# One head's squares, root and scaling placed earlier on ScalarE in the tail of an mLSTM stage

## What is computed

```python
h = mlstm_scan(q, k, vh, i_f, f_f) + flip(mlstm_scan(flip(q), flip(k), flip(vh), flip(i_b), flip(f_b)))
mu = h.mean(-1, keepdims=True)
var = jnp.square(h - mu).mean(-1, keepdims=True)
hn = ((h - mu) * lax.rsqrt(var + LN_EPS)).transpose(0, 2, 1, 3).reshape(B, S, M_WIDTH)
return jax.nn.sigmoid(o_pre) * hn * gn_w
...
y_a = mlstm_branch(...) @ w_a
y_b = dilated_attention(qkv_a, slopes) @ w_b
return (jax.nn.sigmoid(g_a) * y_a + jax.nn.sigmoid(g_b) * y_b) @ w_out
```

## Time and profile before

| | us |
|---|---|
| median of 3 runs | 3447.99 (3446.64 to 3450.39) |
| the profiled execution | 3447.72 |
| its span in the trace | 3446.0 |
| PE busy | 3372.9 (98%) |
| DVE, ACT, POOL busy | 1505.9, 1362.1, 1394.3 (44%, 40%, 40%) |
| mean busy share of the DMA engines | 37.4% (the main queue) |

### The profile page before, as it was taken

The page is one execution under the profiler, slowest core; times in us unless marked ns, Lnnn a source line. Parts: engine busy times, 40 slices in busy tenths (PEclk is TensorE's granted clock), DMA queues, the critical chain, the costliest instruction groups (busy, mean ns, idle before and its releaser), DMA issues.

```text
span 3446.0 us, 39148 instructions
## 1 busy us (share of the span) xinstructions
PE 3372.9 (98%) x15938; PEld 2715.8 (79%) x15938; DVE 1505.9 (44%) x2280; ACT 1362.1 (40%) x2322; POOL 1394.3 (40%) x749
## 2 busy tenths in 40 slices
PE   7999999999999999999999999999999999999999
PEld 5887777887888788777787888876678887778887
DVE  3436663344332343666326433556555402543320
ACT  3545454234232444446323422254632324642321
POOL 2333434444444433344344444442344444134443
PEclk9999999999999999999999999999999999999999
DMA  6334212544554333421244465432135433123332
GB/s 225 104 113 133 62 55 58 153 137 141 177 169 114 109 104 111 135 62 49 84 142 135 147 183 152 111 95 61 49 116 177 139 95 106 37 62 104 98 92 74
DMA packets 566994, 385.31 MB, mean 112 GB/s; under 512 B 13607, under 2 KB 504311, under 8 KB 566815
## 3 DMA queue, kind: packets, MB, share of 16 engines
q1 hardware_dynamic: 564574, 379.58, 37.4%
q10 hardware_dynamic: 2240, 3.25, 0.3%
HBM read 379.27 MB, written 2.10 MB: 111 GB/s over the span
## 4 chain that ended last, share of the span: by engine, by line
PE 92%; DVE 3%; ACT 2%; POOL 1%; DMA 0%; issue 0%; SPq 0%; DVEq 0%; ACTq 0%; POOLq 0%
PE ps L179 91%; PE ps L183 2%; DVE H L154 0%; DVE NUM L146 0%; ACT UF L138 0%; ACT whi L142 0%; DMA W<-in_w_ada 0%; POOL wlo L146 0%; SPq L176 0%; DVE G L163 0%; ACT ox L138 0%; POOL UL L146 0%; ACT L138 0%; DVE HV L150 0%; ACT UH L142 0%
## 5 line engine op out<-in xcount | busy, mean ns | idle before, releaser
L146 POOL TENSOR_TENSOR wlo<-raw,whi 128x1024 fp32r<-128x1024 f32 (+1 forms) x540 | 1256.8, 2336 | 1822.5 <-ACT whi L142 1747.1
L179 PE MATMUL ps<-UH,whi 128*128 128x512 f32 x2656 | 1054.5, 397 | 11.4 <-ACT UH L138 5.6
L179 PE MATMUL ps<-UL,whi 128*128 128x512 f32 x2656 | 1036.1, 391 | 4.0 <-POOL UL L146 3.2
L179 PE MATMUL ps<-UH,wlo 128*128 128x512 f32 x2656 | 1037.6, 391 | 0.5 <-POOL wlo L146 0.5
L142 ACT ACTIVATE whi<-raw 128x1024 fp32r<-128x1024 f32 (+1 forms) x540 | 548.6, 1026 | 744.9 <-PE ps L179 354.4
L179 PEld LDWEIGHTS ps<-UH,whi 128*128 128x128 f32 x2656 | 500.4, 188 | 134.3 <-ACT UH L138 11.4
L179 PEld LDWEIGHTS ps<-UL,whi 128*128 128x128 f32 x2656 | 499.8, 188 | 114.9 <-POOL UL L146 6.6
L179 PEld LDWEIGHTS ps<-UH,wlo 128*128 128x128 f32 x2656 | 500.7, 189 | 107.9 <-issue 3.8
L179 PE MATMUL ps<-GH,whi 128*128 128x512 f32 x704 | 275.3, 391 | 0.0
L179 PE MATMUL ps<-GH,wlo 128*128 128x512 f32 x704 | 274.2, 389 | 0.0
L179 PE MATMUL ps<-GL,whi 128*128 128x512 f32 x704 | 274.0, 389 | 0.0
(11 more groups left out here) (366 smaller groups left out, 4133.2 us busy)
## 6 DMA issues: line engine op xcount, KB each, us to landing
raw<-in_w_in SPq DMA_DIRECT2D x168, 512.0 KB, 3.9
raw<-in_w SPq DMA_DIRECT2D x120, 512.0 KB, 5.3
raw<-in_ada_w SPq DMA_DIRECT2D x96, 512.0 KB, 4.9
raw<-in_w_ada SPq DMA_DIRECT2D x80, 512.0 KB, 4.8
raw<-in_ffn_w_gate SPq DMA_DIRECT2D x44, 512.0 KB, 3.9
raw<-in_ffn_w_up SPq DMA_DIRECT2D x44, 512.0 KB, 3.9
raw<-in_ffn_w_down SPq DMA_DIRECT2D x32, 512.0 KB, 3.9
raw<-in_ev_w_in SPq DMA_DIRECT2D x20, 512.0 KB, 3.8
```

Of the source, the lines that this page charges most:

```text
L146: return self.e.tensor_tensor(o, a, b, op).then_inc(*self.done(*keys))
L179: m = self.e.matmul(o, l, r, start=start, stop=stop)
```

## The change

On ACT, the squares and the root of head 3 are issued right behind that head's `hf`, in sub-step 0 of `it == 4`, ahead of the sigmoids of `og` 5, `ga` 0 and `gb` 0. Heads 0 to 2 keep their place. On DVE the wait for the root, the reciprocal and the scaling of head 3 are written in sub-step 0 instead of 2.

```diff
+        def spread(h):
+            if h:
+                a.wait_ge(*on("dve", "hn", lay, h - 1))
+            for tb in range(4):
+                a.wait_ge(*on("dve", "hv", lay, h, tb))
+                a.af(T["SQ"][:, tb, :], T["HV"][:, tb, :], ACT.Square, ("hq", lay, h), accum_out=T["RS"][:, tb:tb + 1])
+            a.wait_ge(*on("act", "hq", lay, h))
+            a.af(T["RS"], T["RS"], ACT.Sqrt, ("hd", lay, h), scale=1.0 / 256, bias=EPS_LN)
...
                         a.af(T["HV"][:, tb, :], ps(("n", lay, h, tb))[:, 0:256], ACT.Identity, ("hf", lay, h, tb),
                              scale=DN[:, tb:tb + 1])
+                    if h == 3:
+                        spread(h)
...
-                if sub == 1 and h >= 0:
-                    if h:
-                        a.wait_ge(*on("dve", "hn", lay, h - 1))
-                    for tb in range(4):
-                        a.wait_ge(*on("dve", "hv", lay, h, tb))
-                        a.af(T["SQ"][:, tb, :], T["HV"][:, tb, :], ACT.Square, ("hq", lay, h),
-                             accum_out=T["RS"][:, tb:tb + 1])
-                    a.wait_ge(*on("act", "hq", lay, h))
-                    a.af(T["RS"], T["RS"], ACT.Sqrt, ("hd", lay, h), scale=1.0 / 256, bias=EPS_LN)
+                if sub == 1 and 0 <= h < 3:
+                    spread(h)
...
-                if sub == 2 and h >= 0:
+                if sub == (2 if it < 4 else 0) and h >= 0:
                     v.wait_ge(*on("act", "hd", lay, h))
```

## The result

| | before | changed |
|---|---|---|
| median of the runs, us | 3447.97 (3444.92 to 3451.29, 6 runs) | 3427.5 (3425.13 to 3429.23, 6 runs) |
| profiled execution, us | 3447.72 | 3429.23 |
| its span, us | 3446.0 | 3427.5 |

The ratio is 0.994, with a 95% interval of 0.9927 to 0.9952: clearly faster, by 20.5 us between the medians. The forecast was 3427.9, with 20.07 us as the sum of the terms. That the median comes within 0.4 us of it is luck: the interval leaves 16.6 to 25.2 us for the gain.

The account below looks back on a forecast made before the run. The prediction took PE, busy for 98% of the span, to bound the kernel. Savings of 15.12 + 1.58 + 3.37 = 20.07 us off 3447.72 gave 3427.65, stated as 3427.9 for the median, with a range of 3424.5 to 3434.

Parts of the forecast that it names:

- Step 1: From gb 0's last matmul to the first transpose, 7.79 us becomes 0.23 per layer: 15.12 us saved.
- Step 2: From the first transpose to og 6's first matmul, 1.62 us becomes 0.83 per layer: 1.58 us saved.
- Step 3: Block og 6's 24 matmuls fall from 7.01 and 7.42 us to 5.53: 3.37 us saved.
- Step 4: Early squares on ACT make og 5's sigmoid 1.2 us late; gb 0 needs its bank with 3.4 us slack: cost 0.
- Step 5: Roundings queued behind on ACT and POOL: POOL's two parts end near 561.1, PE reaches og 6 at 565.0: cost 0.
- Step 6: DVE's four scalings end at 554.8, PE asks at 564.2: slack 9.4 us, no delay from POOL counted.
- Step 7: DVE's YA and first gate products could each be held by one POOL part, at most 2.34 us: cost 0.
- a loss at the first block with w_a: Gain partly given back where PE reads YAL: 1.8 us wait, twice, giving 3431.5; chance 0.06.
- a clock that does not return: PE's clock does not return or falls elsewhere: 15.1 us saved, 3432.9; chance 0.04.
- another wait in the old one's place: Another PE wait, on a bank or DVE's queue, ends just as late: no change, 3448; chance 0.03.
- The slower one: Squares waiting for DVE's joining block ACT's queue, PE waits at gb 0; loses past 13.4 us of block: 3455; chance 0.02.

Follow-up runs that it names:

- the blocked run: The changed kernel with ACT waiting, ahead of head 3's squares, until PE has made block ga 0: 3442.38 us, ratio to before 0.9986.
- the squares between the sigmoids: The changed kernel with head 3's squares and root moved between the sigmoids of ga 0 and gb 0: 3428.84 us, ratio 0.9942.
- both edits together: The kernel before with PE's transposes behind og 6 and ACT's rounding for ga 1 behind og 6's sigmoid: 3428.99 us, ratio 0.9947.
- the one-layer run: The changed kernel with head 3's squares and root early in layer 0 alone: 3436.98 us, ratio 0.996.

## Why the prediction was right

The forecast, that the stall ends in both layers and everything behind moves up, held, and each term of the sum was measured on its own. By its steps:

- **Step 1, the wait** (15.12). The start of the first transpose is 0.23 behind the last matmul in both layers; 15.12 were saved.
- **Step 2, the transposes** (1.58). They take 562.87 - 562.08 = 0.79, not 0.83: 1.66.
- **Step 3, og 6** (3.37). It takes 568.41 - 562.87 = 5.54, not 5.53: 3.35. The three together are 9.86 in layer 0 and 10.27 in layer 1, 20.13 for a forecast of 20.07.
- **Step 4, og 5's sigmoid**: 1.1 us late (1.2 forecast). `gb` 0 starts at 556.63, 3.5 us after that sigmoid ends (3.4 forecast), and the blocked run shows that this number is the true limit. The Trainium skill's rule in "ScalarE: Activation LUTs", section "What ACT_TABLE_LOAD costs", of a drain on top of the load, is not borne out here: the root starts 1.29 us behind the start of its table load, as before.
- **Step 5, the roundings**: POOL's parts start at 554.14, 7.7 us after `hf`; forecast were 7.8. They are three in a row and not two: a part of 128x512 stood behind the two already before (560.12, 1.28 us), and the prediction left it out. They end 13.7 us after `hf`, 1.1 us later than its 561.1. PE shows no wait for them at `og` 6.
- **Step 6, the scaling**: it ends at 552.60, and PE comes at 562.08. The slack is 9.5 us (9.4 forecast). Of the collision before, the prediction says that the two hold each other up; POOL's part took 2.34 us beside the scaling, no more than its parts of that size beside which DVE was idle (4.75 for two), so only DVE was held there.
- **Step 7**: the two gate products took 3.40 us together, where they had taken 1.28 without POOL beside them, and PE waited for none of it, as argued. Of the four instructions only one was held: the first product took 2.80 us. What reads the products next is ACT's rounding to YAH behind the sigmoid of `og` 7 (575.12), and not that sigmoid.

The rivals: a loss at the first block with w_a is excluded in layer 0 by the rows of YAL and by PE's list of waits, and in layer 1 by the 64 us from `og` 7's first matmul on, which take the same within 0.03 us in both kernels; a clock that does not return, by the 1.00 in the stretches behind and by the same 5.54 us of `og` 6 in layer 1; another wait in the old one's place, by the chain and by the list of PE's waits. The slower one exists as a mechanism, but the joining ends 0.67 us behind `hf` and so nothing blocks; its break-even point of 13.4 us was too far off (about 11, see the blocked run).

One thing the spans alone would have hidden: they differ by 18.5 us, not 20.1. The changed kernel's first trace was 2.1 us ahead before the first tail and lost 3.6 behind the second. Both are of the size by which traces of one and the same kernel differ (1.7 us ahead of the tail between the two of before, 1.9 behind it between the two of the changed kernel). The medians, which differ by 20.5, agree with the tails. Matched matmul by matmul, the 3.6 us lie in three places: 1.4 us in the 45.0 us from 2241 on in the trace of before, 1.6 in the 42.0 us from 2358 on, and 1.1 in the 23.1 us from 2912 on, where the wait for KD lies; the rest gives 0.6 back. The first two stand in the second trace of the changed kernel too, with a mean granted clock of 0.85 and 0.84 instead of 0.89 and 0.88. The end of the stall does not bring them: the squares between the sigmoids and both edits together, which have no long stall either, take 45.1 and 44.5 us in the first place and 40.4 in the second, so no more than before within 0.1. Whether the new order on ACT has a part in them is not shown; the medians leave little room for it.

## What to carry to other kernels

When the bounding engine waits, follow the chain back and ask for each link when its inputs were ready: here they had been ready 14 us before, and only the order of an in-order queue held them. To move work ahead in such a queue, price what it pushes back (here one sigmoid that frees a PSUM bank, with 3.4 us of slack) and add what the stall costs afterwards: a quarter of this gain was matmuls at the lower clock. Being ready just in time is worth as much as being early, but a margin of some us guards against neighbours such as POOL's part in the scaling.

## What was not expected of the hardware

- The clock can fall after the work has resumed. Behind a wait of 1.98 us it read 1.00 during the wait, 0.98 in the next 1.5 us, and 0.50 only after that, with PE busy; the cost came in `og` 7, behind the transposes, and was 1.6 us. Behind 0.87 us it did not fall, behind 5.3 and 7.4 us it read 0.50 from the first matmul on, or close to it.
- What a stall costs in clock varied with the kernel and the place. Behind a wait of 5.27 us `og` 6 took 0.9 to 1.0 us more, behind 7.40 in most traces 1.5 to 1.9 and in the one-layer run 2.1 (7.66 us); the transposes ahead of it took 0.83 us more each time, which makes 1.7 to 1.8 and 2.3 to 2.9 us in all. In the blocked run no transposes lie between, and `gb` 0 alone took 2.5 and 2.2 us more behind 5.31.
- A DVE instruction that meets one of POOL's can be held until about the end of that one, and not only the scaling: the two products with two inputs in SBUF took 3.40 us beside POOL's 2.40, and 1.28 us alone. Not every instruction is held: in the same trace the product `sg<-sg,ps`, which has one input in PSUM, ran in its usual 0.69 us at 590.44, while POOL worked from 587.61 to 592.38. The Trainium skill's "Advanced Engine Details and Errata", section "VectorE Performance Modes", names two-port instructions on the one side and GpSimd on the other; the scaling, 1.14 us without POOL and 3.28 or 2.17 with it, agrees. The rows of the product that was not held, POOL's first and then its own:

```profile
587.61 4.77 POOL L146 TENSOR_TENSOR wlo<-raw,whi 128x1024 fp32r<-128x1024 f32 x2
590.44 0.69 DVE L146 TENSOR_TENSOR sg<-sg,ps 128x512 f32<-128x512 f32 x1 [2.35 <-PE ps L179]
```
